# A fused two-block model on one core: small work of the first mixer and of the routing placed between larger groups

## What is computed

```python
def first_block(x, mem, ...):                      # DEPTH = 1
    x = x + parallel_mixer(rms_norm(x, g_mix), ...)        # mLSTM heads (both directions) and a gated MLP side by side
    x = x + memory_cross_attention(rms_norm(x, g_xattn), rms_norm(mem, g_mem), ...)
    x = x + hier_moe(rms_norm(x, g_moe), ...)              # 32 experts: best of 4 groups, then top 2 of its 8
    return rms_norm(x, g_final)

def hier_moe(h, ...):
    g_idx = top_k(softmax(h @ w_rg + b_rg), 1)
    e_top, e_local = top_k((h @ w_re + b_re)[g_idx], 2)
    weights = p_top * softmax(e_top)
    # every row goes through its two experts: (silu(x @ w_gate[e]) * (x @ w_up[e])) @ w_down[e], weighted and added

def second_block(x, ...):                          # DEPTH_2 = 2: hyena, gated linear attention and pooling, then a wide MLP
```

## Time and profile before

| | us |
|---|---|
| median of 3 runs | 1829.97 |
| lowest and highest | 1829.95, 1832.75 |
| profiled execution, its own time | 1833.16 |
| its span | 1831.0 |
| TensorE matmul busy | 1752.5 (96%) |
| VectorE busy | 543.5 (30%) |
| ScalarE busy | 269.0 (15%) |
| DMA moved | 398.90 MB, mean 218 GB/s |

### The profile page before, as it was taken

One profiled execution on the slowest core, in us unless ns is written; L12 is line 12 of the kernel. 1 busy time (PEld: TensorE's weight loads), 2 busy tenths in 40 slices (PEclk: granted clock), 3 DMA queues, 4 the chain that ended last, 5 costly groups with the idle time before them and its releaser, 6 DMA issues.

```text
span 1831.0 us, 20842 instructions
## 1 busy us (share of the span) xinstructions
PE 1752.5 (96%) x9018; PEld 1199.3 (66%) x9018; DVE 543.5 (30%) x1137; ACT 269.0 (15%) x593; POOL 25.2 (1%) x49
## 2 busy tenths in 40 slices
PE   7999998979898899899999999999999999999998
PEld 7476755424344344497788788874786888698853
DVE  4323114344334333334420232210326122322201
ACT  2222121000000000214310021000114110110100
POOL 0010000000000000000000000000000000000000
PEclk9989997989989899899999999999999999999999
DMA  8422554999999999933234324352443233434160
GB/s 340 162 112 93 219 240 184 382 427 427 428 427 427 428 427 426 392 139 134 96 138 161 138 109 168 138 211 108 167 155 138 93 138 123 170 143 184 64 235 23
DMA packets 30124, 398.90 MB, mean 218 GB/s; under 512 B 3472, under 2 KB 3792, under 8 KB 5584
## 3 DMA queue, kind: packets, MB, share of 16 engines
q1 hardware_dynamic: 29456, 394.54, 53.5%
q10 hardware_dynamic: 576, 3.01, 0.4%
HBM read 396.49 MB, written 1.05 MB: 217 GB/s over the span
## 4 chain that ended last, share of the span: by engine, by line
PE 90%; DMA 5%; DVE 3%; issue 1%; ACT 0%; SPq 0%; POOL 0%; DVEq 0%; ACTq 0%
PE bank L1102 89%; DMA zone<-in_w_experts 3%; DMA w<-in_w_experts 2%; PE bank L1146 2%; DMA w<-in_w_first 1%; DVE zone L2172 0%; DVE x L2295 0%; ACT zone L1602 0%; DVE zone L2203 0%; DVE zone L2179 0%; DVE const L2256 0%; DVE zone L2113 0%; DVE zone L2114 0%; ACT zone L1584 0%; DVE zone L2184 0%
## 5 line engine op out<-in xcount | busy, mean ns | idle before, releaser
L1102 PE MATMUL bank<-zone,w 128*128 128x256 f32 (+1 forms) x4224 | 815.1, 356 | 7.6 <-DMA w<-in_w_first 2.8
L1102 PEld LDWEIGHTS bank<-zone,w 128*128 128x128 f32 x4224 | 727.7, 192 | 96.4 <-issue 12.2
L1102 PE MATMUL bank<-w,zone 128*128 128x512 f32 (+1 forms) x1760 | 510.1, 619 | 13.3 <-DMA w<-in_w_experts 9.1
L1102 PEld LDWEIGHTS bank<-w,zone 128*128 128x128 f32 (+1 forms) x1760 | 203.8, 156 | 291.3 <-issue 282.8
L1102 PE MATMUL bank<-zone 128*32 128x512 f32 (+10 forms) x2344 | 347.2, 460 | 16.3 <-DMA zone<-in_w_experts 6.4
L1102 PEld LDWEIGHTS bank<-zone 128*128 128x128 f32 (+4 forms) x2344 | 200.7, 159 | 162.2 <-issue 123.8
L1611 ACT ACTIVATE zone<-bank 128x512 f32<-128x512 f32 (+2 forms) x145 | 81.4, 575 | 663.6 <-PE bank L1102 553.7
L2781 DVE TENSOR_SCALAR zone<-zone,vec 128x256 f32<-128x256 f32 x68 | 28.1, 414 | 256.7 <-ACT zone L2638 256.7
L2638 ACT ACTIVATE zone<-bank 128x256 f32<-128x256 f32 x68 | 24.9, 384 | 321.2 <-PE bank L1102 321.2
L1146 PE MATMUL bank<-const,zone 128*128 128x128 f32 (+2 forms) x268 | 41.2, 293 | 27.7 <-DVE zone L2172 11.5
L1146 PEld LDWEIGHTS bank<-const,zone 128*128 128x128 f32 (+2 forms) x268 | 32.8, 154 | 49.4 <-DVE zone L2266 16.8
(11 more groups left out here) (246 smaller groups left out, 592.0 us busy)
## 6 DMA issues: line engine op xcount, KB each, us to landing
w<-in_w_layers SPq DMA_DIRECT2D x68, 2048.0 KB, 7.8
w<-in_w_experts SPq DMA_DIRECT2D x52, 2048.0 KB, 22.0
zone<-in_w_experts SPq DMA_DIRECT2D x44, 2048.0 KB, 24.3
w<-in_w_first SPq DMA_DIRECT2D x16, 2048.0 KB, 8.4
w<-in_w_layers SPq DMA_DIRECT2D x6, 1024.0 KB, 5.3
zone<-in_row ACTq DMA_DIRECT2D x2, 1024.0 KB, 4.7
zone<-in_table SPq DMA_DIRECT2D x1, 1536.0 KB, 11.3
const<-in_const SPq DMA_DIRECT2D x1, 1153.0 KB, 12.8
```

Of the source, the lines that this page charges most:

```text
L1102: return eng.matmul(out, lhsT, rhs, start=start, stop=stop, **kw_)
```

## The change

- **Start.** SyncE issues the first tile of x, the identity, the vector table, then the left 256 columns of each 512 of slot q, then x's second tile, then the right columns. `tall_by_tiles` starts on the left half (`ld_left`) and takes the slot's own signal only for its second pair of groups.
- **Row broadcasts.** `gcol` moves ahead of o; `mu0`, `mu1` follow o's two groups, `mu2`, `mu3` follow kx0's.
- **Norm by tiles.** y's first tile is transposed inside vx0's second group, before its step 6, y's second tile inside out's first group, before its step 4.
- **Transposes two steps sooner.** In `widest` the next norm's first tile is transposed before step 4 of the last group and not before step 6.
- **Routing.** `rank` becomes one bank for each tile. VectorE ranks and picks tile 0 in the middle of `choose(1)`, and TensorE gathers tile 0 for pass 0 before tile 1 is ranked. Both `weigh` and `Pw` move into pass 0, behind the scaling of `in1`, the register loads, the first two copies of `more_slot` and `more_rows`. In all passes the transposes of `Pw` move behind gate block 1, ahead of `more_in`, and the copy `more_slot(1)` ahead of `weights` and the next pass's `place`.

```diff
-        def tall_by_tiles(pl, pre, act, norm, n):
-            k, w = slot(pl)
+        def tall_by_tiles(pl, pre, act, norm, n, left=None):
+            if left is None:
+                k, w = slot(pl)
             for g in range(2):
+                if left is not None:
+                    if g == 0:
+                        eng.wait_ge(*pl.need(left, 16))
+                        w = spots[FIRST_RING[0]]
+                    else:
+                        k, w = slot(pl)
                 early(pl, f"{pre}{g}", (w, w), (2 * g * P, (2 * g + 1) * P), act, 0)
...
-                        if (n, t, c) == (1, 1, 6):
+                        if (n, t, c) == (1, 1, 4):
                             norm_tile_T(pl, norm, hs, sem("hs"), n_hs, 0)
...
+            wide(pl, "o", hT, also=lambda t: row_of(t))
+            for evacuated in banks.taken_up(pl, *[f"nm{g}" for g in range(4)]):
+                eng.wait_ge(*evacuated)
+            tall(pl, "kx0", hmT, 4, also=lambda g: row_of(2 + g))
...
-            wide(pl, "vx0", hmT)
-            norm_T(pl, "ny", y, sem("y"), 2)
-            for evacuated in banks.taken_up(pl, *[f"ny{g}" for g in range(4)]):
-                eng.wait_ge(*evacuated)
-            widest(pl, "out", hT, "nq", 5)
+            k, w = slot(pl)
+            for t in range(TT):
+                bank = opened(pl, f"vx0{t}")
+                for c in range(KT):
+                    if (t, c) == (1, 6):
+                        norm_tile_T(pl, "ny", y, sem("y"), 1, 0)
...
+            for evacuated in banks.taken_up(pl, "ny0", "ny1"):
+                eng.wait_ge(*evacuated)
+            def second_rows():
+                norm_tile_T(pl, "ny", y, sem("y"), 2, 1)
+            widest(pl, "out", hT, "nq", 5, second=(second_rows, "ny2", "ny3"))
...
+            gather(0)
+            eng.wait_ge(*pl.need(sem("assigned"), 2))
+            mm(rank1[:, 0:NE], up_to, asg[:, 1, :], False, False, skip_group_check=True)
+            mm(rank1[:, NE:2 * NE], every, asg[:, 1, :], False, True, skip_group_check=True).then_inc(*banks.close(pl, "rank1"))
+            gather(1)
...
                     release(at)
                     if (kind, c) == ("gate", 1):
+                        eng.wait_ge(*pl.need(sem("placed"), 1 if pass0 else 0))
+                        transposes(pl, "weights", [(P, t * P, P, Pw[:, t, :], ident) for t in range(TT)])
                         eng.wait_ge(*pl.need(sem("more_picked"), 1))
...
+            choose(pl, 0)
+            choose(pl, 1, lambda: ranked(0))
+            ranked(1)
...
+            if i == 0:
+                eng.wait_ge(*pl.own(vstep))
+                q, e = choice()
             more_slot(pl, q, 0)
+            if i == 0:
+                eng.wait_ge(*pl.need(sem("w_used0"), 1))
+            more_slot(pl, q, 1)
+            if i == 0:
+                more_rows(pl, e)
+                for t in range(TT):
+                    weigh(pl, t)
+                weigh_rows(pl, 0)
             eng.wait_ge(*banks.filled_up(pl, "weights"))
...
+            rows(0)
             eng.dma_start(const[:, 0:P], dram["const"][:, 0:P]).then_inc(*pl.up(sem("ld_ident"), 16))
             eng.dma_start(vec1, dram["vec1"]).then_inc(*pl.up(sem("ld_vec1"), 16))
...
+            eng.dma_start(*left).then_inc(*pl.up(sem("ld_left"), 16))
+            rows(1)
+            eng.dma_start(*right).then_inc(*pl.up(sem(f"w_ready{FIRST_RING[0]}"), 16))
```

More of the change, by code:

```diff
@@ L450 @@
            'picked': 1,
-           'placed': 1,
-           'taken0': 3,
-           'taken1': 3,
+           'placed': 2,
+           'taken0': 2,
+           'taken1': 2,
            'taken2': 2,
@@ L1216, in wide, with widest @@
                                                        for c in range(kt)])])
+                if also is not None:
+                    also(t)
             release(k)
-        def widest(pl, pre, act, norm, n_hs, ready=None):
+        def widest(pl, pre, act, norm, n_hs, ready=None, second=None):
             two = []
@@ L1398, in expert_pass @@
         def expert_pass(pl):
-            eng.wait_ge(*pl.need(sem("picked"), 0))
-            for g in range(2):
-                group(pl, f"in{g}", [((P, j * P, P), [(hs[:, t, (4 * g + j) * P:(4 * g + j + 1) * P], Pe[:, t, :])
-                                                      for t in range(TT)]) for j in range(4)])
-            eng.wait_ge(*pl.need(sem("placed"), 0))
-            transposes(pl, "weights", [(P, t * P, P, Pw[:, t, :], ident) for t in range(TT)])
+            pass0 = pl.region == PASS[0]
+            if pass0:
+                gp = gathering[0]
+            else:
+                gp = pl
+                eng.wait_ge(*pl.need(sem("picked"), 0))
+                for g in range(2):
+                    group(pl, f"in{g}", [((P, j * P, P), [(hs[:, t, (4 * g + j) * P:(4 * g + j + 1) * P], Pe[:, t, :])
+                                                          for t in range(TT)]) for j in range(4)])
             def more_slot(n):
@@ L2041, in first, with ranked, choose @@
                 evac_T(pl, "ne", hT, None, "g_moe", [t])
[L2042 to L2043 removed]
+            def ranked(t):
+                eng.wait_ge(*banks.filled_up(pl, f"rank{t}"))
+                eng.wait_ge(*pl.own(sem("assigned")))
+                ins = V.tensor_tensor(rank[:, t, :], banks.tile(pl, f"rank{t}")[:, 0:NE], asg[:, t, :], ALU.mult)
                 if t == 0:
[L2045 to L2054 removed]
+                    ins.then_inc(*banks.done(pl, "rank0"))
+                    for evacuated in banks.taken_up(pl, "rank0"):
+                        eng.wait_ge(*evacuated)
+                else:
+                    v(pl, ins)
+                pick(0, t).then_inc(*pl.up(sem("first_picked")))
+            choose(pl, 0)
+            choose(pl, 1, lambda: ranked(0))
+            ranked(1)
+            gathering.append(pl)
+            V.tensor_copy(tot, banks.tile(pl, "rank1")[:, NE:2 * NE]).then_inc(*banks.done(pl, "rank1"))
+            for evacuated in banks.taken_up(pl, "rank1"):
                 eng.wait_ge(*evacuated)
[L2057 removed]
+        gathering = []
+        def choose(pl, t, meanwhile=None):
             eng.wait_ge(*banks.filled_up(pl, f"route{t}"))
@@ L2076, in choose @@
                                          expert.rearrange("p (g e) -> p g e", g=NG), ALU.mult, ALU.add))
+            if meanwhile is not None:
+                meanwhile()
             v(pl, V.max(best, em[:, 32 * t:32 * t + 32]))
@@ L2244, in expert_pass @@
                     ins.then_inc(*pl.up(vstep))
-            ins.then_inc(*banks.done(pl, "in1"))
+            ins.then_inc(*banks.done(gp, "in1"))
+            if i == 0:
+                eng.wait_ge(*pl.own(vstep))
+                q, e = choice()
             more_slot(pl, q, 0)
+            if i == 0:
+                eng.wait_ge(*pl.need(sem("w_used0"), 1))
+            more_slot(pl, q, 1)
+            if i == 0:
+                more_rows(pl, e)
+                for t in range(TT):
+                    weigh(pl, t)
+                weigh_rows(pl, 0)
             eng.wait_ge(*banks.filled_up(pl, "weights"))
```

141 lines of the change are left out of this document (75 added, 66 removed).

## The result

| | before | after |
|---|---|---|
| median | 1830.15 us (9 runs, 1828.56 to 1832.75) | 1835.83 us (9 runs, 1835.42 to 1838.64) |
| profiled execution, its own time | 1833.16 us | 1835.42 us |
| its span | 1831.0 us | 1833.2 us |

The ratio is 1.0030, 95% interval 1.0019 to 1.0040: the changed kernel is 5.7 us slower. The forecast was 1829.4, within 0.2% of before, and the time lies above the range.

What follows compares the result with a forecast made beforehand. The prediction took the expert stage's full DMA pipe as the bound, its end moving with slot 11's issue at 321.48 us. Terms 1.3 - 5.2 + 0.2 - 1.45 + 4.6 = -0.55 us gave 1829.4 us, range 1824.8 to 1834.0.

Steps and rivals of the forecast that it cites:

- A: Start: x's second tile comes behind the half slot while VectorE waits for both tiles, so the first projection starts +1.3 us.
- B: Row broadcasts spread between projection groups: the clock stays up where it had fallen at 118 to 128 us, -5.2 us.
- C: Norm by tiles, between vx0 and out: transposes and idle take 3.2 us in all against 3.0, +0.2 us.
- D: Transposes two steps sooner: TensorE's 1.44 us idle after out goes, -1.45 us.
- E: Routing, with xo's edit: TensorE waits 3.4 us for `placed`, more_in runs at 1.2 GHz, slot 11 goes +4.6 us.
- x's second tile arrives 1 MB later: 3.1 us: Start: x's second tile stands behind a 1 MB half slot, priced at the slot's own rate, 3.1 us.
- The bound of +4: Start: upper case, +4 us if the 1 KB pieces of the halves run at half the rate.
- each broadcast (0.85 us at 2.4 GHz): Row broadcasts: each one, standing between projection groups of 6.9 us, takes 0.85 us at 2.4 GHz.
- rival 3: Mixer: the broadcasts are not what takes the clock, so their gain is missing, 1834.6 us; chance 0.05.
- Rival 2: Expert pipe: 1.2 GHz lasts into the up projection, late filter weights leave a hole of some 4.5 us, 1836 us; chance 0.12.
- Rival 1: Routing gain goes through: 2.4 GHz in more_in and third gate block, 1825.1 us, or 1821 with fast gather; chance 0.28.

Runs made afterwards that it cites:

- e9: Kernel before with the new start alone, ScalarE and VectorE taking each x tile when it is there; 1828.7 us, ratio 0.9989.
- e2: Kernel before with the row broadcasts between projection groups alone; 1829.0 us, ratio 0.9993.
- e11: Kernel before with only the twelve tiny transposes moved ahead of o, the four broadcasts still together behind kx0; 1829.3 us, ratio 0.9998.
- e3: Kernel before with the new routing alone; 1835.8 us, ratio 1.0035.
- e1: Kernel before with the new start alone (half slots, x's second tile behind the left half); 1835.0 us, ratio 1.0027.
- e4: Changed kernel without its new start and new routing; 1825.2 us, ratio 0.9973 against the kernel before.
- e5: e3 with both weigh steps moved into VectorE's idle time before tile 1's rank, Pw behind the second pick; 1829.8 us, ratio 1.0003 against before.
- e6: e5 with the two register loads back behind fullest; 1828.3 us, ratio 0.9992 against before.
- e8: Kernel before with the new start alone, but x's second tile issued ahead of the left half again; 1828.0 us, ratio 0.9993.
- e7: Kernel before with the filter table ahead of slot 10 and the small filter loads behind pass 1's third slot; 1828.4 us, ratio 0.9991.
- e10: Kernel before with row broadcasts, both norm edits, e6's routing and e7's queue order, old start; 1823.2 us, ratio 0.9959.

## Why the prediction was wrong

**What bounds the kernel: right.** The forecast rested on the rule that the end moves as slot 11's issue moves. It moved 4.14 us and the last slot 5.12. In the eleven profiles with the old place of the table the time between the two is 428.8 to 430.5 us, whatever stood before it. The 1 us more that the changed kernel has over before is inside that spread. And from the last landing to the end of the span all fourteen profiles need 1077.2 to 1080.1 us, while the landing itself lies between 741.4 and 756.0.

**The sum was 4.7 us short at slot 11** (+4.14 measured, -0.55 forecast). Of the 6.2 us between the forecast change and the measured one (+5.7 by the medians) that is the main part; 1.0 more came between slot 11 and the last landing, and the rest is within the interval. By terms, as the two traces have them:

| term | forecast | measured | from |
|---|---|---|---|
| A, start | +1.3 | +3.74 | gates, 29.39 to 33.13 |
| B, broadcasts | -5.2 | -3.49 | offset +3.74 at the gates, +0.25 at the scores (142.13 to 142.38) |
| C, norm by tiles | +0.2 | +0.2 | vx0 to out's last groups |
| D, transposes at out | -1.45 | -1.56 | offset -1.11 at qx0 |
| E, routing and xo | +4.6 | +5.25 | offset at slot 11, 4.14 + 1.11 |

- **A failed, by 2.4 us, and it is the step "x's second tile arrives 1 MB later: 3.1 us".** It arrives 5.1 us later (10.84 instead of 5.74): the left half lands 4.4 us behind the vector table, not 3.1, and the two small tables, now also ahead of x's second tile, take 1.0 more (x's first tile is in at 4.21, the vector table at 5.18), which the forecast put at nothing; the first tile's landing 0.2 us sooner gives a little back. Of these 5.1, 1.9 are the old wait for the slot, as forecast. So 2.0 of the 2.4 us are the arrival. The other 0.5 are the first group, 6.04 us instead of 5.53, with the first rise of the clock at 20.24 instead of 15.94 us; that part is a draw, since in the nine profiles with the old start the gates lie between 28.67 and 30.30, and before's 29.39 is an early one. The mechanism (two tiles waited for) was right, e9 shows it. The bound of +4, given for halves at half the rate, was the nearer end.
- **B was too large by 1.7 us: the step "each broadcast (0.85 us at 2.4 GHz)".** It takes 1.06, and the projection groups beside it 7.06 and 7.10 instead of 6.87 and 6.96: 1.25 or 1.20 apiece, 1.5 too much in all. That the clock stays up was right. The Trainium skill, "TensorE: Matmul & The Clock Gate", Part 1, has the gate follow how busy TensorE has been. By it rival 3 would have held; e2 and e11 speak against it, since in before and in e11 TensorE was busy for 10.00 of 10.00 us while the clock fell, and only the broadcasts' place decides.
- **C and D were right** to 0.1 us, the idle of 1.18 us ahead of out among them.
- **E was nearly right**, 0.65 us short, from two misses of opposite sign: xo gives 1.7 us (offset -2.78 at the rank), not 1, and the routing itself costs 6.9 (32.62 us from rank to slot 11 against 25.70), not 5.6. e3, without xo's edit, has 6.4 from rank to slot 11 and 6.4 in the time. The mechanism came as told: 3.4 us of standing were forecast, 3.67 came, with more_in at 1.2 GHz behind it. What was not seen is that the wait is all of E's cost, and that a gap for the weights lay ahead of it.
- **The base was off too.** The sum was made against a profiled execution 3.2 us over the median and carried over unchanged. But B was priced on it, where the fall of the clock behind the broadcasts lasted 10.2 us; in other profiles it is 6.8 (below), so an ordinary run had less to win. The times of the parts add up within their error: +4.9 (e1), +6.4 (e3) and -4.9 (e4, which is B, C, D and the same edit at xo) make +6.4, and the changed kernel has +5.5 (3.5 to 7.3) by its ratio.

Rival 2's number, 1836, was hit, but not by its mechanism: there is no hole, the filter loads came 8.6 us behind slot 11. Rival 1 needed 2.4 GHz in more_in. e5 shows what it would have given: with the wait gone the routing costs nothing.

**What the new profile was to show**: clock 1.00 from 90 to 140 us, 1.2 us of idle before out, none after it, over 3 us ahead of the weight transposes: all there. First projection at 13 to 14 us, slot 11 at 320 to 322, last slot at 749 to 752: 15.57, 325.62 and 756.03, all wrong: the first by A alone, the other two by A and B, with 0.65 us from E. The row that was to name VectorE's Pw multiply as the end of the wait says "issue".

## What to carry to other kernels

Find the point from which a full queue sets the end, and price every edit ahead of it by that point alone: here 1 us at 13 us of the program is 1 us at its end. When a load is split so that work can start on its first part, look who waits for the thing that is now behind that part; the waits have to be split with it. And work that is pushed behind something needs a look at where its reader stands in TensorE's queue: the same instructions in an idle gap of VectorE's were free, behind the copies they cost 6.7 us, more than half of it by the clock.

## What was not expected of the hardware

- **The same instructions lose the clock for different times.** In nine profiles with the four broadcasts together the fall lasted 10.2 us in four (before, e1, e6, e8), 6.8 in four (e3, e5, e7, e11) and 3.4 in one (e9). The Trainium skill, "TensorE: Matmul & The Clock Gate", Part 1, says that the gate's measure runs freely and does not start with the kernel, so where a change falls depends on its phase; the nine profiles agree. In the nine profiles with the old start the first rise of the clock lies anywhere between 15.06 us (e10) and 18.02 (e5). A gain that is read from one profile's low clock is read from one draw.
- **Two halves of a slot are not as fast as the slot.** The whole slot is in at 12.20 us, behind both tiles of x; in halves of 1 KB pieces, with one tile of x between them, the same bytes are in at 14.10, and in e8, in halves behind both tiles of x, at 13.05. The first half moved 1 MB in 4.4 us (3.8 in e8), the second, behind a busy queue, in 3.3 (3.0 in e8), the whole slot 2 MB in 6.1.
- **SyncE's issue behind the halves is slow**: the small table's takes 2.86 us (4.22 to 7.08) where it took 0.43. No one waits for SyncE there.
- **A wait on TensorE costs twice**: 3.7 us of standing in e3 and 3.1 more in the 32 records of more_in behind it, since the clock falls 2.3 us into the wait.
